# Seven pairs per down projection in layers two to four, with four of the seven weight sums built by adding transfers

## The chip, the cores and the metric

The kernel runs on one core of one Trainium2 chip. The metric is the device time of one execution in microseconds (us), lower is better. Three runs of the kernel before gave a median of 1669.83 us (1669.68 to 1669.99).

## The reference, cut to what matters

The input is 256 tokens of width 1024 in float32. Two blocks follow each other. The first holds four feed-forward layers (counted from 0 in the code: layers 0 to 3), with a state-space mixer between layers 0 and 1 and a neighbourhood attention between layers 2 and 3. Each feed-forward layer is

```
def swiglu(x, w_gu, w_down):
    g, u = jnp.split(x @ w_gu, 2, axis=-1)
    return (jax.nn.silu(g) * u) @ w_down
...
h = h + 0.5 * swiglu(rmsnorm(h, ffn1_norm[i]), ffn1_w_gu[i], ffn1_w_down[i])
```

with `w_gu` of 1024 x 5632 and `w_down` of 2816 x 1024. The change concerns the product with `w_down` (the down projection) of layers 1, 2 and 3.

## The kernel before, in words

**Numbers.** Every float32 product is made of three matmuls of halves: an operand x is split into a rounded part (`hi`) and the rest (`lo`), and hi\*hi + hi\*lo + lo\*hi is summed in PSUM. Weights are loaded from HBM in tiles of up to 2048 columns on 128 partitions (1 MB) into one of four slots of `raw` (`NRAW = 4`). For each tile ScalarE (ACT) writes `whi`, then VectorE (DVE) writes `wlo = raw - whi`; each has three slots (`NSPL = 3`). TensorE (PE) then multiplies. All tiles stand in one list (`plan_of`), and every engine goes through that list in order. ACT may convert tile n once PE has given back tile n-3 (event `w_rel`), and PE needs `wlo` of tile n. SyncE (SP) loads the raw slots in the same order; a slot is free when `w_hi` and `w_lo` of its last tile are done.

**The down projection.** The 2816 rows are 22 blocks of 128 (k), the 1024 columns two halves (c), the 256 tokens two halves (t). An ordinary tile ("rest", label `("down", i, c, y)`) holds up to four blocks k of one column half; each block needs two products of 128x512 (one per t), so six matmuls. A *pair* j takes the blocks 2j and 2j+1 in both column halves, a 2 by 2 block product, by a seven-product scheme (`seven`): 7 products, 21 matmuls, where the plain way takes 8 products, 24 matmuls. For that, sums of weight blocks are needed: the tile `paired` (P_j below; three blocks of the weights themselves, 1536 columns, three products, 9 matmuls) and the tile `mixed` (M_j; three sums of blocks and one block, 2048 columns, four products, 12 matmuls). DVE makes the sums of M_j in `sums`, three dependent additions into a buffer `ts`, just ahead of its `wlo` of P_j. The activations need differences too: POOL makes them (`differences` into `dsum`) in the up projection, and ACT and DVE split them into `dThi` and `dTlo`.

Each layer uses four pairs (blocks 0 to 7). `down_tiles` sets the order: rest (0,0), P0, M0, rest (1,0), P1, M1, rest (0,1), P2, M2, rest (1,1), P3, M3, rest (0,2), and three closing tiles. Between two pairs there is thus an ordinary tile of 24 matmuls (12 after the last pair). The up projection ahead of it runs over 11 chunks of 256 columns, each two tiles of 24 matmuls.

**State space.** Between layers 0 and 1, `w_in` of the mixer passes through 32 tiles (`SSD_TILES`). POOL adds six blocks of squares (`ssd`, into `gate`) late in this stage, and PE reads their total in `square_rows`.

Of the kernel before, what the change touches and what calls it, by code (L numbers as in the profile page):

```python
# [20 lines left out]
PAIRS = 4  # L21
# [141 lines left out]
def plan_of(dr):  # L163
    p = Plan()

    def ffn(i, up, down, extra=None):
        for c in range(11):
            if extra is not None and c in (0, 2):
                p.add(("pproj", extra, c // 2), [wsrc(dr["ple_w_proj"][extra], 0, 2, c * 256, 512)], 2, 512)
            for k in range(2):  # L170
                p.add(("up", i, c, k), [wsrc(up, 4 * k, 4, x * 2816 + c * 256, 256) for x in range(2)], 4, 512)

        def rest(c, y):
            k0, nk = DOWN_TILES[c, y]
            p.add(("down", i, c, y), [wsrc(down, k0, nk, c * 512, 512)], nk, 512)

        for what, x in DOWN_ORDER:
# [5 lines left out]
        for x in DOWN_LAST:  # L183
            rest(*x)
# [78 lines left out]
DOWN_ORDER, DOWN_TILES, DOWN_LAST = down_tiles(PAIRS)  # L263
# [130 lines left out]
def programs(dr, mem, banks, plan, ev):  # L394
# [26 lines left out]

    def wsource(n):

        if labels[n][0] == "mixed":
            return mem[f"ts{labels[n][2] % 3}"][:, :]
        return mem["raw"][:, plan.raw_of[n] % NRAW, columns_of_tile(n)]

    def landed(n):

        if labels[n][0] == "mixed":  # L430
            return at("tsum", *labels[n][1:])
        return at(f"d_w{plan.raw_of[n] % NRAW}", n)
# [120 lines left out]
    def sync(S):  # L553
# [67 lines left out]
    def tensor(T):  # L621
# [203 lines left out]
        def mixed_down(i, r, turn_last):  # L825
# [17 lines left out]
            def rest(c, y):  # L843
                k0, nk = DOWN_TILES[c, y]
# [10 lines left out]
            def seven(j):  # L855
                first, final = j == 0, j == PAIRS - 1
# [19 lines left out]
            for what, x in DOWN_ORDER[1:]:  # L876
# [6 lines left out]
            closing_block([("down", i) + DOWN_LAST[0]], (6, 7), aThi, aTlo, DOWN_TILES[DOWN_LAST[0]][0])  # L883
            residual_in(r, 0, (6, 7))
            held, k0 = [], DOWN_TILES[DOWN_LAST[1]][0]
            for x in DOWN_LAST[1:]:
                hi, lo = take("down", i, *x)
                held += [(hi[:, k, :], lo[:, k, :]) for k in range(DOWN_TILES[x][1])]
            T.wait_ge(*at("aTlo", i, 10))
            for t in range(2):  # L890
                for k, (hi, lo) in enumerate(held):
# [7 lines left out]
                    if t and k == DOWN_TILES[DOWN_LAST[1]][1] - 1:  # L899
                        last.then_inc(*sig(*named(("down", i) + DOWN_LAST[1])))  # L900
                last.then_inc(*sig(*half(("down", i) + DOWN_LAST[2], t)))
# [637 lines left out]
    def scalar(A):  # L1539
# [71 lines left out]
        def ffn(i, r, extra=None):  # L1611
            fa, aThi = mem["fa"], mem["aThi"]

            def high_a(c):
                A.wait_ge(*at("turn_a", i, c))
                b = banks[4 + c % 2]
                if c >= PAIRS:
# [15 lines left out]
            def mixed_down(r):  # L1633
                take("down", i, 0, 0)
                high_a(10)
                for what, x in DOWN_ORDER[1:]:
# [5 lines left out]
                A.wait_ge(*at("w_rel", "paired", i, PAIRS - 1))  # L1642
                copy(flat(mem["ftmp"][:, :, :]), banks[0], scale=0.5).then_inc(*sig("root", i))
                take("down", i, *DOWN_LAST[0])
                take("down", i, *DOWN_LAST[1])
# [5 lines left out]
                take("down", i, *DOWN_LAST[2])  # L1651
# [6 lines left out]
            for c in range(11):  # L1658
# [15 lines left out]
                if 1 <= c <= PAIRS:  # L1674
# [451 lines left out]
    def vector(V):  # L2126
# [8 lines left out]
        def sums(n):  # L2135
# [9 lines left out]
            else:  # L2145
                V.wait_ge(*at("dTlo", i, PAIRS - 1))
# [71 lines left out]
        def ffn(i, r, extra=None):  # L2218
            fa, aThi, aTlo = mem["fa"], mem["aThi"], mem["aTlo"]

            def low_a(c):
                V.wait_ge(*at("aThi", i, c))
                b = banks[4 + c % 2]
                if c >= PAIRS:
# [12 lines left out]
            def merged():  # L2237
# [4 lines left out]
                V.wait_ge(*at("w_rel", "mixed", i, PAIRS - 1))  # L2242
# [8 lines left out]
            def mixed_down(r):  # L2251
                take("down", i, 0, 0)
                low_a(10)
                for what, x in DOWN_ORDER[1:]:
# [5 lines left out]
                take("down", i, *DOWN_LAST[0])  # L2260
                merged()
                V.wait_ge(*at("h21", i))
                for t in range(2):
                    residual(r, t, 0, half(("down", i) + DOWN_LAST[0], t), 6 + t, 0.5)
                take("down", i, *DOWN_LAST[1])
                early_quarters(r)
                V.wait_ge(*at("h22", i))
                for t in range(2):
                    residual(r, t, 1, half(("down", i) + DOWN_LAST[2], t), 2 + t, 0.5)
# [5 lines left out]
                take("down", i, *DOWN_LAST[2])  # L2275
# [7 lines left out]
            for c in range(11):  # L2283
# [14 lines left out]
                if 1 <= c <= PAIRS:  # L2298
# [487 lines left out]
    def gpsimd(G):  # L2786
# [85 lines left out]

        def ffn(i, extra=None):
# [12 lines left out]
        rstds(1)  # L2886
        ssd()
# [8 lines left out]
        ffn(3, 1)  # L2896
        rstds(7)
# [8 lines left out]
def layout(nc):  # L2906
# [44 lines left out]
    put("dThi", [P, PAIRS, 3, P], F32R, a0)  # L2951
    put("dTlo", [P, PAIRS, 3, P], F32R, z + 56 * 1024)
# [108 lines left out]
```

## Time and profile before

| | |
|---|---|
| median of three runs | 1669.83 us |
| the profiled execution | 1669.54 us, of which the span is 1667.7 us |
| mean granted clock of TensorE | 0.998 |
| PE busy | 99% of the span |
| DVE, ACT, POOL busy | 70%, 56%, 8% |
| bytes read from HBM | 297.96 MB |
| down projections of layers 0 to 3 | from about 137, 603, 811 and 1121 us, some 60 us each |
| up projection of layer 0; state-space stage | before 137 us; about 196 to 470 us |

The span is the profiled part of the execution; 1.84 us lie around it. PE's busy time is the union of its matmuls, whose ends are modelled and overlap, so a short wait of PE shows as less idle time than it costs; the starts of successive matmuls tell its pace.

### The profile page before, as it was taken

The page shows a single profiled execution, that of the slowest core. Times are in us where ns is not written, and L with a number is a line of the kernel's source. Part 1 is how long each engine was busy: PE and PEld are TensorE (multiplying, and loading weights), DVE is VectorE, ACT ScalarE, POOL GpSimd, SP SyncE. Part 2 cuts the span into 40 slices and gives each one's busy share as a digit, 9 for nine tenths or more (in the row PEclk, how much of TensorE's full clock was granted, in tenths as well). Part 3 has the DMA queues.
Part 4 walks back from the last instruction along what each step waited for, and adds up shares of the span by engine and source line. Part 5 has one row for each costly group of instructions (what it writes and reads, how often), then busy time and mean ns, then how long its engine had stood idle before and what let it go on. Part 6 is the DMA issues. An engine that isn't in the chain of part 4 may idle for free.

```text
span 1667.7 us, 23289 instructions
## 1 busy us (share of the span) xinstructions
PE 1655.8 (99%) x9318; PEld 1416.7 (85%) x9318; DVE 1161.4 (70%) x1500; ACT 940.5 (56%) x1363; POOL 125.1 (8%) x135
## 2 busy tenths in 40 slices
PE   8999999999999999999999999999999999999998
PEld 7888899999788888888888778888889999988886
DVE  5657878999966568765688767567855578776643
ACT  6545566777865445754456666545653556564532
POOL 0100000000111000010007401000000000000000
PEclk9999999999999999999999999999999999999999
DMA  9654677676556646656487336655655533465551
GB/s 302 194 183 164 186 187 208 180 196 207 161 190 197 195 158 204 200 178 194 159 228 244 114 111 205 190 184 163 220 182 165 161 102 127 156 210 178 177 195 57
DMA packets 244235, 300.58 MB, mean 180 GB/s; under 512 B 9505, under 2 KB 175777, under 8 KB 244129
## 3 DMA queue, kind: packets, MB, share of 16 engines
q1 hardware_dynamic: 238480, 289.26, 54.6%
q10 hardware_dynamic: 5648, 9.85, 2.4%
q8 instruction: 74, 1.21, 0.3%
q14 instruction: 33, 0.26, 0.0%
HBM read 297.96 MB, written 1.11 MB: 179 GB/s over the span
## 4 chain that ended last, share of the span: by engine, by line
PE 98%; DVE 1%; DMA 0%; ACT 0%; issue 0%; DVEq 0%; ACTq 0%
PE bank L625 95%; PE bank L628 4%; DMA prm<-in_prm 0%; DVE wlo L2130 0%; ACT hThi L1546 0%; DVE rTlo L2133 0%; DVE hTlo L2133 0%; DVE xn L2133 0%; DVE h L2133 0%; ACT rThi L1546 0%; DVE xn L2200 0%; DVEq L2988 0%; ACT xn L1543 0%; ACT whi L1546 0%; ACTq L2086 0%
## 5 line engine op out<-in xcount | busy, mean ns | idle before, releaser
L2130 DVE TENSOR_TENSOR wlo<-raw,whi 128x2048 fp32r<-128x2048 f32 (+2 forms) x284 | 613.5, 2165 | 231.1 <-ACT whi L1546 231.1
L1546 ACT ACTIVATE whi<-raw 128x2048 fp32r<-128x2048 f32 (+2 forms) x284 | 511.7, 1810 | 167.1 <-PE bank L625 162.7
L625 PE MATMUL bank<-whi,hThi 128*128 128x512 f32 x1056 | 420.8, 398 | 0.5 <-ACT whi L1546 0.5
L625 PE MATMUL bank<-wlo,hThi 128*128 128x512 f32 x1056 | 412.4, 390 | 0.4 <-DVE wlo L2130 0.4
L625 PE MATMUL bank<-whi,hTlo 128*128 128x512 f32 x1056 | 396.9, 391 | 0.0
L625 PE MATMUL bank<-hThi,whi 128*128 128x256 f32 x888 | 253.4, 285 | 0.0
L625 PE MATMUL bank<-hThi,wlo 128*128 128x256 f32 x888 | 251.2, 283 | 0.0
L625 PE MATMUL bank<-hTlo,whi 128*128 128x256 f32 x888 | 251.2, 283 | 0.0
L625 PEld LDWEIGHTS bank<-whi,hThi 128*128 128x128 f32 x1056 | 198.8, 188 | 44.8 <-issue 5.8
L625 PEld LDWEIGHTS bank<-whi,hTlo 128*128 128x128 f32 x1056 | 198.6, 188 | 42.4
L625 PEld LDWEIGHTS bank<-wlo,hThi 128*128 128x128 f32 x1056 | 198.8, 188 | 40.3 <-DVE wlo L2130 1.5
L625 PEld LDWEIGHTS bank<-hThi,whi 128*128 128x128 f32 x888 | 169.5, 191 | 3.8 <-issue 3.3
L625 PEld LDWEIGHTS bank<-hTlo,whi 128*128 128x128 f32 x888 | 169.5, 191 | 0.2
L625 PEld LDWEIGHTS bank<-hThi,wlo 128*128 128x128 f32 x888 | 169.5, 191 | 0.2
L625 PE MATMUL bank<-whi,aThi 128*128 128x512 f32 x288 | 113.6, 395 | 0.4
L625 PE MATMUL bank<-whi,aTlo 128*128 128x512 f32 x288 | 112.2, 390 | 0.0
L625 PE MATMUL bank<-wlo,aThi 128*128 128x512 f32 x288 | 112.1, 389 | 0.0
L1543 ACT ACTIVATE ftmp<-bank,st 128x256 f32<-128x256 f32 x88 | 41.5, 476 | 101.5 <-PE bank L625 101.5
L2130 DVE TENSOR_TENSOR aTlo<-bank,aThi 128x512 fp32r<-128x512 f32 (+2 forms) x60 | 29.3, 511 | 78.5 <-ACT aThi L1546 78.5
L1546 ACT ACTIVATE aThi<-bank 128x512 fp32r<-128x512 f32 (+2 forms) x60 | 25.5, 457 | 98.3 <-PE bank L628 98.3
L2790 POOL TENSOR_TENSOR st<-st,cst 128x1 f32<-128x1 f32 (+2 forms) x35 | 36.9, 1068 | 458.6 <-DVE st L2173 433.5
L1546 ACT ACTIVATE hThi<-bank,prm 128x128 fp32r<-128x128 f32 (+1 forms) x152 | 43.4, 379 | 47.5 <-PE bank L628 42.4
(245 smaller groups left out, 2157.0 us busy)
## 6 DMA issues: line engine op xcount, KB each, us to landing
raw<-in_ffn_w_gu SPq DMA_DIRECT2D x172, 512.0 KB, 4.8
raw<-in_w_in SPq DMA_DIRECT2D x30, 1024.0 KB, 5.1
raw<-in_ffn_w_down SPq DMA_DIRECT2D x24, 1024.0 KB, 5.1
raw<-in_ffn_w_down SPq DMA_DIRECT2D x40, 512.0 KB, 4.0
raw<-in_ssd_w_in SPq DMA_DIRECT2D x16, 1024.0 KB, 5.7
raw<-in_ssd_w_in SPq DMA_DIRECT2D x32, 512.0 KB, 5.6
raw<-in_w_up SPq DMA_DIRECT2D x16, 1024.0 KB, 5.4
raw<-in_w_down SPq DMA_DIRECT2D x16, 1024.0 KB, 5.1
```

The source lines that it names most:

```text
L625: return T.e.matmul(out, lhsT, rhs, start=start, stop=stop, skip_group_check=skip)
L628: return T.e.transpose(out, in_, ident)
L1543: return e.activation(out, in_, func, **kw)
L1546: return e.activation(out, in_, ACT.Identity, **kw)
L2130: return e.tensor_tensor(out, a, b, op)
L2790: return e.tensor_tensor(out, a, b, op)
```

## The change

`PAIRS` becomes a tuple: layer 0 keeps four pairs, layers 1 to 3 have seven (blocks 0 to 13). `down_tiles` then leaves one ordinary tile in front (rest (0,0), blocks 14 to 17), one of half size (rest (1,0), blocks 14 and 15) after pair 0, and pairs 1 to 6 stand one after the other.

For the pairs in `AHEAD` (1, 2, 4 and 5 of each of the three layers) DVE makes no sums. A new tensor `mix` in HBM holds them; POOL fills it by six transfers for each pair (`mix`: three copies and three transfers with `accum_op` add, each waiting for the one before), 72 in all, one at each "beat": 10 in the up projection of layer 0, 30 in the state-space stage (ahead of POOL's own sums there), and 11, 11 and 10 in the up projections of layers 1 to 3. SP loads such an M_j from `mix` into a raw slot as one transfer of 1 MB, and of P_j only the three blocks that are used (0.75 MB instead of 1 MB). For pairs 0, 3 and 6 DVE still makes the sums, all three in `ts0`.

```
-PAIRS = 4
+PAIRS = (4, 7, 7, 7)
+AHEAD = ((), (1, 2, 4, 5), (1, 2, 4, 5), (1, 2, 4, 5))
+BEATS = (range(1, 11), range(11), range(11), range(11))
+SSD_BEATS = (1, 31, 1)
+MIX = [(i, j) for i in range(4) for j in AHEAD[i]]
...
-                p.add(("mixed", i, x), None, 4, 512)
+                p.add(("mixed", i, x), [dr["mix"][i, x]] if x in AHEAD[i] else None, 4, 512)
...
+    def summed_here(n):
+        return labels[n][0] == "mixed" and labels[n][2] not in AHEAD[labels[n][1]]
...
-                if labels[m][0] == "paired":
+                if labels[m][0] == "paired" and summed_here(m + 1):
                     S.wait_ge(*at("tsum", *labels[m][1:]))
+            if labels[n][0] == "paired" and not summed_here(n + 1):
+                e.dma_start(slot[:, 1:2, 0:512], pieces[0][:, 1:2, :]).then_inc(*sig(f"d_w{q % NRAW}", n, by=16))
+                e.dma_start(slot[:, :, 512:1024], pieces[1]).then_inc(*sig(f"d_w{q % NRAW}", n, by=16))
+                return
+            if labels[n][0] == "mixed":
+                S.wait_ge(*at("m_step", *labels[n][1:], 5))
...
-                if labels[n][0] == "paired":
+                if labels[n][0] == "paired" and summed_here(n + 1):
                     sums(n)
...
+        def mix(i, j, step):
...
+            if step == 0:
+                done = e.dma_start(target[:, 0:2, :], block(0, 1).to_broadcast([P, 2, 512]))
+            elif step == 1:
+                done = e.dma_start(target[:, 0:2, :], diagonal, accum_op=ALU.add)
+            elif step == 2:
+                done = e.dma_start(target[:, 2:3, :], target[:, 0:1, :])
+            elif step == 3:
+                done = e.dma_start(target[:, 2:3, :], block(1, 1), accum_op=ALU.add)
+            elif step == 4:
+                done = e.dma_start(target[:, 3:4, :], target[:, 2:3, :])
+            else:
+                done = e.dma_start(target[:, 3:4, :], block(1, 0), accum_op=ALU.add)
+            done.then_inc(*sig("m_step", i, j, step, by=16))
...
+        def mix_at(n):
+            b = next(beats, None)
+            if b is not None:
+                G.wait_ge(*at("w_hi", n))
+                if b:
+                    G.wait_ge(*at("m_step", *steps[b - 1]))
+                mix(*steps[b])
...
         def ffn(i, extra=None):
-            for c in range(PAIRS):
-                differences(i, c)
+            for c in range(11):
+                if c < PAIRS[i]:
+                    differences(i, c)
...
+                if c in BEATS[i]:
+                    mix_at(tile["up", i, c, 0])
...
         rstds(1)
+        for k in range(*SSD_BEATS):
+            mix_at(tile[SSD_TILES[k]])
         ssd()
```

On DVE, in the middle of a down projection of layers 1 to 3, the rows before read as follows (from M0 on: M0, the fresh column `aTlo`, rest (1,0), the sums and `wlo` of pair 1, `wlo` of M1, rest (0,1)).

```order
L2130 TENSOR_TENSOR wlo<-ts_74,whi 128x2048
L2130 TENSOR_TENSOR aTlo<-bank,aThi 128x512
L2130 TENSOR_TENSOR wlo<-raw,whi 128x2048
L2130 TENSOR_TENSOR ts_75<-raw 128x1024
L2130 TENSOR_TENSOR ts_75<-ts_75,raw 128x512 x2
L2130 TENSOR_TENSOR wlo<-raw,whi 128x1536
L2130 TENSOR_TENSOR wlo<-ts_75,whi 128x2048
L2130 TENSOR_TENSOR wlo<-raw,whi 128x2048
```

The same place now, from `aTlo` on: rest (1,0), pairs 1 and 2 without sums, the sums of pair 3, P3, M3, then P4.

```order
L2143 TENSOR_TENSOR aTlo<-bank,aThi 128x512
L2143 TENSOR_TENSOR wlo<-raw,whi 128x1024
L2143 TENSOR_TENSOR wlo<-raw,whi 128x1536
L2143 TENSOR_TENSOR wlo<-raw,whi 128x2048
L2143 TENSOR_TENSOR wlo<-raw,whi 128x1536
L2143 TENSOR_TENSOR wlo<-raw,whi 128x2048
L2143 TENSOR_TENSOR ts_74<-raw 128x1024
L2143 TENSOR_TENSOR ts_74<-ts_74,raw 128x512 x2
L2143 TENSOR_TENSOR wlo<-raw,whi 128x1536
L2143 TENSOR_TENSOR wlo<-ts_74,whi 128x2048
L2143 TENSOR_TENSOR wlo<-raw,whi 128x1536
```

The sums of an inner pair now stand between two pairs instead of behind an ordinary tile of 2048 columns.

On POOL, from the end of layer 0 through the state-space stage, only the six sums stood before, after the last additions of the layer and the norm.

```order
L2790 TENSOR_TENSOR h<-h,ftmp 128x512
L2790 TENSOR_TENSOR h<-h,fa 128x512
L2790 TENSOR_TENSOR st<-st,cst 128x1 x2
L2790 TENSOR_TENSOR gate<-gate 128x512 x6
L2790 TENSOR_TENSOR st<-st,cst 128x2
```

Now 30 transfers stand between the norm and the sums; these are the last six of them and what follows.

```order
L2902 DMA mix<-mix 128x512
L2904 DMA mix<-in_ffn_w_down 128x512
L2894 DMA mix<-in_ffn_w_down 128x2x512
L2896 DMA mix<-in_ffn_w_down 128x2x512
L2898 DMA mix<-mix 128x512
L2900 DMA mix<-in_ffn_w_down 128x512
L2803 TENSOR_TENSOR gate<-gate 128x512 x6
L2803 TENSOR_TENSOR st<-st,cst 128x2
```

POOL's sums are now behind all 30 transfers in its queue.

## Rows read from the trace of the kernel before

**Rows 1.** The page, part 1: busy us, share, instructions of each engine.

```profile
PE 1655.8 (99%) x9318; PEld 1416.7 (85%) x9318; DVE 1161.4 (70%) x1500; ACT 940.5 (56%) x1363; POOL 125.1 (8%) x135
```

**Rows 2.** Busy us by stretch: layer 1's down stage, its up stage, state space.

```profile
core 0: us, PE busy (x) PEld busy (x) DVE busy (x) ACT busy (x) POOL busy (x), PEclk, DMA share, GB/s
...
603.00:663.00 60.00, 59.88 (x270) 49.02 (x269) 48.06 (x47) 32.42 (x31) 3.00 (x2) 1.00 0.58 193
...
560.00:600.00 40.00, 40.00 (x186) 33.09 (x185) 22.39 (x18) 17.50 (x18) 0.00 (x0) 1.00 0.58 191
...
200.00:411.00 211.00, 210.91 (x1714) 205.55 (x1714) 189.91 (x299) 150.25 (x233) 0.55 (x1) 1.00 0.69 193
```

**Rows 3.** Timeline of PE in layer 1's down stage: start, us, engine, line, operation.

```profile
613.47 0.39 PE L625 MATMUL bank<-whi,aTlo 128*128 128x512 f32 x1
613.98 0.47 PE L625 MATMUL bank<-whi,aThi 128*128 128x512 f32 x1
614.29 0.39 PE L625 MATMUL bank<-wlo,aThi 128*128 128x512 f32 x1
...
616.14 0.39 PE L625 MATMUL bank<-whi,aThi 128*128 128x512 f32 x1
...
619.54 0.39 PE L625 MATMUL bank<-whi,aThi 128*128 128x512 f32 x1
...
624.07 0.39 PE L625 MATMUL bank<-whi,aTlo 128*128 128x512 f32 x1
```

**Rows 4.** Timeline of DVE in the same stage.

```profile
611.54 2.29 DVE L2130 TENSOR_TENSOR wlo<-raw,whi 128x2048 fp32r<-128x2048 f32 x1 [1.11 <-ACT whi L1546]
613.75 1.22 DVE L2130 TENSOR_TENSOR ts<-raw 128x1024 f32<-128x1024 f32 x1
615.00 1.42 DVE L2130 TENSOR_TENSOR ts<-ts,raw 128x512 f32<-128x512 f32 x2
616.34 1.75 DVE L2130 TENSOR_TENSOR wlo<-raw,whi 128x1536 fp32r<-128x1536 f32 x1
...
621.75 2.29 DVE L2130 TENSOR_TENSOR wlo<-raw,whi 128x2048 fp32r<-128x2048 f32 x1 [1.05 <-ACT whi L1546]
```

**Rows 5.** Timeline of ACT in the same stage.

```profile
609.60 3.28 ACT L1546 ACTIVATE whi<-raw 128x2048 fp32r<-128x2048 f32 x2
616.45 1.92 ACT L1546 ACTIVATE whi<-ts 128x2048 fp32r<-128x2048 f32 x1 [3.57 <-DVE ts L2130]
619.80 3.54 ACT L1546 ACTIVATE whi<-raw 128x2048 fp32r<-128x2048 f32 x2 [1.43 <-PE bank L625]
621.84 1.50 ACT L1546 ACTIVATE whi<-raw 128x1536 fp32r<-128x1536 f32 x1
```

**Rows 6.** The busiest 10 us of the transfers, and issues with median us to landing.

```profile
870.00:880.00 10.00, 10.00 (x50) 8.26 (x49) 5.56 (x13) 6.61 (x15) 1.07 (x2) 1.00 1.04 374
...
raw<-in_ffn_w_down SPq DMA_DIRECT2D x24, 1024.0 KB, 5.1
raw<-in_ffn_w_down SPq DMA_DIRECT2D x40, 512.0 KB, 4.0
...
tb<-in_rpb SPq DMA_DIRECT2D x2, 1000.0 KB, 14.1
...
out<-xn SPq DMA_DIRECT2D x4, 256.0 KB, 2.1
```

**Rows 7.** State space: ACT's second and thirty-first tile, POOL's sums, PE's read of them.

```profile
199.84 1.93 ACT L1546 ACTIVATE whi<-raw 128x2048 fp32r<-128x2048 f32 x1
...
380.07 1.90 ACT L1546 ACTIVATE whi<-raw 128x2048 fp32r<-128x2048 f32 x1
...
411.10 1.29 POOL L2790 TENSOR_TENSOR gate<-gate 128x512 f32<-128x512 f32 x1 [209.64 <-DVE EW L2130]
...
457.02 3.21 POOL L2790 TENSOR_TENSOR gate<-gate 128x512 f32<-128x512 f32 x1 [3.97 <-ACT gate L1543]
...
465.24 1.50 PE L625 MATMUL bank<-cst,gate 128*128 128x2 f32 x13
```

More of the change, by code:

```diff
@@ L173, in rest @@
         def rest(c, y):
-            k0, nk = DOWN_TILES[c, y]
+            k0, nk = DOWN_TILES[i][c, y]
             p.add(("down", i, c, y), [wsrc(down, k0, nk, c * 512, 512)], nk, 512)
-        for what, x in DOWN_ORDER:
+        for what, x in DOWN_ORDER[i]:
             if what == "rest":
@@ L855, in seven @@
             def seven(j):
-                first, final = j == 0, j == PAIRS - 1
+                first, final = j == 0, j == PAIRS[i] - 1
                 hi, lo = take("paired", i, j)
@@ L875, in mixed_down @@
             clear(0, 1, 2, 3, 5)
-            for what, x in DOWN_ORDER[1:]:
+            for what, x in DOWN_ORDER[i][1:]:
                 if what == "rest":
@@ L882, in mixed_down @@
                 empties[b] = (event, i)
-            closing_block([("down", i) + DOWN_LAST[0]], (6, 7), aThi, aTlo, DOWN_TILES[DOWN_LAST[0]][0])
+            closing_block([("down", i) + DOWN_LAST[i][0]], (6, 7), aThi, aTlo, DOWN_TILES[i][DOWN_LAST[i][0]][0])
             residual_in(r, 0, (6, 7))
-            held, k0 = [], DOWN_TILES[DOWN_LAST[1]][0]
-            for x in DOWN_LAST[1:]:
+            held, k0 = [], DOWN_TILES[i][DOWN_LAST[i][1]][0]
+            for x in DOWN_LAST[i][1:]:
                 hi, lo = take("down", i, *x)
-                held += [(hi[:, k, :], lo[:, k, :]) for k in range(DOWN_TILES[x][1])]
+                held += [(hi[:, k, :], lo[:, k, :]) for k in range(DOWN_TILES[i][x][1])]
             T.wait_ge(*at("aTlo", i, 10))
@@ L898, in mixed_down @@
                         turn(1, 0, 1)
-                    if t and k == DOWN_TILES[DOWN_LAST[1]][1] - 1:
-                        last.then_inc(*sig(*named(("down", i) + DOWN_LAST[1])))
-                last.then_inc(*sig(*half(("down", i) + DOWN_LAST[2], t)))
+                    if t and k == DOWN_TILES[i][DOWN_LAST[i][1]][1] - 1:
+                        last.then_inc(*sig(*named(("down", i) + DOWN_LAST[i][1])))
+                last.then_inc(*sig(*half(("down", i) + DOWN_LAST[i][2], t)))
             residual_in(r, 1, (2, 3))
@@ L1635, in mixed_down @@
                 high_a(10)
-                for what, x in DOWN_ORDER[1:]:
+                for what, x in DOWN_ORDER[i][1:]:
                     if what == "rest":
@@ L1650, in mixed_down @@
                     high(1, 0, 1)
-                take("down", i, *DOWN_LAST[2])
+                take("down", i, *DOWN_LAST[i][2])
                 if r == 1:
@@ L2253, in mixed_down @@
                 low_a(10)
-                for what, x in DOWN_ORDER[1:]:
+                for what, x in DOWN_ORDER[i][1:]:
                     if what == "rest":
@@ L2259, in mixed_down @@
                     take("mixed", i, x)
-                take("down", i, *DOWN_LAST[0])
+                take("down", i, *DOWN_LAST[i][0])
                 merged()
@@ L2263, in mixed_down @@
                 for t in range(2):
-                    residual(r, t, 0, half(("down", i) + DOWN_LAST[0], t), 6 + t, 0.5)
-                take("down", i, *DOWN_LAST[1])
+                    residual(r, t, 0, half(("down", i) + DOWN_LAST[i][0], t), 6 + t, 0.5)
+                take("down", i, *DOWN_LAST[i][1])
                 early_quarters(r)
@@ L2268, in mixed_down @@
                 for t in range(2):
-                    residual(r, t, 1, half(("down", i) + DOWN_LAST[2], t), 2 + t, 0.5)
+                    residual(r, t, 1, half(("down", i) + DOWN_LAST[i][2], t), 2 + t, 0.5)
                     if r == 1 and t == 0:
@@ L2274, in mixed_down @@
                     scaled(0)
-                take("down", i, *DOWN_LAST[2])
+                take("down", i, *DOWN_LAST[i][2])
                 if r == 1:
@@ L2871, in differences @@
             tt(d[:, 384:512], a[:, 256:384], d[:, 256:384], ALU.subtract).then_inc(*sig("dsum", i, c))
+        def mix(i, j, step):
+            w = dr["ffn1_w_down" if i % 2 == 0 else "ffn2_w_down"][i // 2]
+            block = lambda k, c: w[256 * j + 128 * k:256 * j + 128 * k + 128, 512 * c:512 * c + 512].unsqueeze(1)
+            first = block(0, 0)
+            diagonal = bass.AP(first.tensor, first.offset, [[D, P], [P * D + 512, 2], [1, 512]])
+            target = dr["mix"][i, j]
+            if step == 0:
[11 more added lines that the diff above has]
+            done.then_inc(*sig("m_step", i, j, step, by=16))
+        steps = [(i, j, step) for i, j in MIX for step in range(6)]
+        beats = iter(range(len(steps)))
+        def mix_at(n):
[5 more added lines that the diff above has]
+                mix(*steps[b])
         def ffn(i, extra=None):
-            for c in range(PAIRS):
-                differences(i, c)
+            for c in range(11):
+                if c < PAIRS[i]:
+                    differences(i, c)
                 if c == 2 and extra is not None:
                     ple_rstd(extra)
+                if c in BEATS[i]:
+                    mix_at(tile["up", i, c, 0])
             G.wait_ge(*at("h12p", i))
@@ L2896, in gpsimd @@
         ffn(3, 1)
+        assert next(beats, None) is None
         rstds(7)
```

38 lines of the change are left out of this document (20 added, 18 removed).

## The prediction

> **What bounds the kernel now.** I read the page first: PE is busy 99% of the span, the other engines 70% and less [rows 1]. So the time falls only by what PE no longer does, and rises by every wait that PE gets. Next the busy time by stretch: in layer 1's down stage PE is busy 59.88 of 60 us, DVE 48.06 and ACT 32.42 [rows 2]; the stages of layers 2 and 3 read alike. The reader should see that DVE has only a fifth of this stage free, while in the up stage it has nearly half (22.39 of 40 us). Last the timelines of the three engines in this stage, because an average hides which wait ends last.
>
> PE's pace comes from starts: from 616.14 to 624.07 us there are 35 steps without a wait, 0.2266 us each [rows 3]. (The 0.39 us of a row is the length of one pipelined matmul, not the pace.) A pair of 21 matmuls thus takes 4.76 us, its P_j 2.04, its M_j 2.72, an ordinary tile of 24 takes 5.44.
>
> **What is removed.** Nine more pairs (three in each of three layers) save three matmuls each: 27 x 0.2266 = 6.1 us, all of it on PE, so on the path. A second, small gain: in the stage before, the matmul due at 613.70 (613.47 + 0.23) starts at 613.98, and the next follows after 0.31 instead of 0.23 [rows 3]. This is rest (1,0), whose conversion could start on ACT only at 609.60 [rows 5] and ended on DVE at 611.54 + 2.29 = 613.83 [rows 4]. The tile now has half the columns; at half the durations (an estimate: 0.96 on ACT, 1.15 on DVE) it would be ready near 611.8. That removes 0.28 + 0.08 = 0.36 us per layer, 1.1 us in three.
>
> **What is moved: the sums between two pairs.** This is the step on which I decide. Between two pairs there was an ordinary tile of 5.44 us of PE work; from pair 1 to pair 6 there is none. Take the latencies from the rows: ACT starts 0.26 us after PE's next tile has started (619.54 to 619.80), converts 2048 columns in 1.92, DVE starts 0.03 later and its next instruction follows 2.21 after (611.54 to 613.75); the sums take 2.59 (613.75 to 616.34); `wlo` of P takes 1.75; PE starts 0.15 after `wlo` (613.83 to 613.98) [rows 3 to 5].
>
> Count from the moment when PE ends P1. M2 is three tiles behind P1, so ACT may convert it then: 0.26 + 1.92 + 0.03 + 2.21 = 4.42 when DVE is free. DVE takes its instructions in order, and behind `wlo` of M2 stand the sums of pair 3: to 7.01. Then `wlo` of P3: to 8.76; PE could start P3 at 8.91. PE has only M1, P2 and M2 to do meanwhile, 33 x 0.2266 = 7.48. P3 comes 1.43 us late, with 0.08 for the restart 1.51. Next M3: ACT can start it when the sums are done, 2.70 after they began (616.45 - 613.75), at 7.12; + 1.92 + 0.03 + 2.29 + 0.15 = 11.51. PE would have reached it at 8.99 + 2.04 = 11.03: late by 0.48, with the restart 0.56. One inner summed pair thus costs 2.07 us. Pair 6 stands in the same place behind pairs 4 and 5; pair 0 keeps its place. Two per layer, six in all: 12.4 us.
>
> What is late next: P4 and M4 are converted behind M3, but PE is then late itself, and the same count leaves them 1.2 and 0.7 us to spare. Behind pair 6 comes a tile whose conversion may start well before, and PE's wait gives ACT and DVE time.
>
> A pair summed ahead must hold pace too. M_j may be converted when P_(j-1) ends: 0.26 + 1.92 + 0.03 + 2.29 + 0.15 = 4.65 us, against 4.76 of PE work: 0.11 to spare. P_j: 0.26 + 1.50 + 0.03 + 1.75 + 0.15 = 3.69 against 4.76. Both hold, M_j barely: if the latencies were 0.1 longer than read, each could cost up to 0.1, all twelve 1.2 us.
>
> **What is added elsewhere, at no cost.** In the up stage three more chunks per layer get POOL's differences and their split; ACT has 22 and DVE 18 of 40 us free there [rows 2]. The beats in the up stages come once per chunk, 48 x 0.2266 = 10.9 us apart, so POOL waits for a step only if it takes longer; then the differences, ACT's split and what is queued behind it on ACT would be late. SP's wait for the last step of a pair would hold up all weight loads behind it, but the steps end stages earlier; only in layer 3 are the last ones issued in its own up stage, two chunks and half a down stage ahead. SP's table for the attention now waits for M6 of layer 2 instead of M3, which comes about when the slot for the next load is freed anyway.
>
> **The loads.** A pair summed ahead needs 0.75 + 1 MB (1.835 million bytes) in 4.76 us, 385 GB/s; the highest rate over 10 us was 374 [rows 6], and this stage itself moved 193 GB/s at a share of 0.58 [rows 2], 333 when busy. So four slots must bridge. The tightest is M2: its slot is rest (1,0)'s, free near 611.9 on the old stage's clock; ACT wants M2 when P1 ends, at 613.70 + 21 x 0.2266 (rest (1,0) and P1) + 0.26 = 618.7. That is 6.8 us for a load that takes 5.1 [rows 6]. The summed pairs need only 1 MB in more than 6 us. I take no wait; the price if that is wrong is 1.835/333 or /374 against 4.76: 0.75 or 0.15 us for each of twelve pairs, 9.0 or 1.8 us.
>
> The Trainium skill's page "DMA: Bandwidth & Descriptors" (Specifications) gives 358 GB/s as the limit of HBM for a core. By that an ahead pair takes 5.13 us, 4.4 us more in twelve if nothing were buffered, and the sum would be 1679.4. The 374 GB/s of the trace is over this limit, so the trace decides.
>
> **The steps in the state-space stage.** The trace has no adding transfer. Its nearest rows: 2.1 us for a 256 KB store below, 14.1 us for the slowest load of 1000 KB above [rows 6]. The steps move 256 or 512 KB, and an adding one reads as much again; the rows nearest to this are the loads of 512 KB (4.0) and 1 MB (5.1). I take 5. What they must meet: the first can be issued at 201.8 (second tile's `whi`), and the thirtieth's gate falls at 382 [rows 7]. POOL's six sums come behind, five of 1.29 and one of 3.21, 9.7 us, and PE reads them at 465.2 [rows 7]. So 29 steps have till 455.5: 8.75 us each. At 5 they just follow the tiles and cost nothing; above 8.75, each us costs 29. Weight loads have a share of 0.69 there and DVE is busy 190 of 211 us [rows 2], but the steps take nothing from DVE.
>
> By the Trainium skill's page "DMA: Bandwidth & Descriptors" (Anatomy of one DMA — SWDGE (gpsimd) path), a transfer issued by POOL takes 2.0 us + bytes/436e3, by estimate 2.6 and 3.2 us for the two sizes; by it the sum stays as it is. No row of this trace shows it.
>
> **The sum.** - 6.1 - 1.1 + 12.4 = + 5.2 us. On the profiled 1669.54 that gives 1674.7; the median is 0.29 higher, so 1675.0 for a median. A change is told from none here at 0.2%, 3.3 us.
>
> **The rivals.**
> - *Loads fall behind as well* (14%): the 385 GB/s are not bridged. For it: the demand is above every rate of the trace. Against: 1.7 us to spare in the tightest place. 1677 to 1684.
> - *The waits are half as long* (14%): then + 6.2 - 7.2 = - 1.0, about 1669, no change. For it: they are differences of long chains, 8.91 against 7.48. Against: the latencies agree from place to place.
> - *The sums find room and the gain is kept* (10%): the mechanism is that DVE has pair 3's sums done before PE needs P3; it decides at a chain of 7.48 us instead of 8.91, if DVE could have M2's `wlo` behind it 1.4 us sooner. Then - 7.2, 1662.6. For it: DVE's work for pairs 1 to 6, 4 x 3.96 + 2 x 6.55 = 28.9 us (2.21 + 1.75 each, 2.59 more with sums), nearly fits into PE's 28.6. Against: three slots don't let it work ahead.
> - *The steps are late in the state-space stage* (6%): at 10 us each + 36 us, near 1711.
> - The forecast has 56%; its own range is 1673 to 1677 (from waits of 1.8 to 2.4 us per inner summed pair), of which 6 points lie within 0.2%.
>
> Faster 10%, same 14 + 6 = 20%, slower 70%. The range from 1669.5 to 1682 leaves out the kept gain, the late steps and the far end of late loads, some 20%.
>
> **What would show it.** In the new timeline PE should wait near 1.4 us before P3 and P6 and 0.5 before M3 and M6 in layers 1 to 3, released by `wlo`, and not before pairs 1, 2, 4, 5; DVE's sums should begin the moment `wlo` of the tile ahead ends. Pace and matmul count: 27 matmuls fewer at 0.2266. Steps should land within 4 to 7 us, and POOL's sums end before 455. The prediction is wrong if PE waits for transfers, or if `wlo` comes before PE asks for it.

## The result, and the profile after

The changed kernel takes 1683.79 us (median of 4 runs, 1680.80 to 1685.09) against 1669.76 (1668.97 to 1669.99) of the kernel before: a ratio of 1.0082 [1.0068, 1.0096], slower by 14.0 us. The forecast was 1675.0 with a range to 1682: the direction is right, the size is 8.8 us too small and outside the range. The profiled execution is the fastest of the four, 1680.80 us with a span of 1679.0, 11.3 us above the one of before. In the table further down, single executions far above the rest (2350 us of steps alone, 5344 of fetch later, three of the kernel before beside some of the runs) are left out of the ratios, and move no median by more than 0.15 us.

The page of the kernel after, part 1, and in part 3 the queue of POOL's transfers (packets, MB, share), which before did not exist:

```profile
PE 1654.0 (99%) x9291; PEld 1412.8 (84%) x9291; DVE 1179.1 (70%) x1527; ACT 963.2 (57%) x1408; POOL 191.8 (11%) x234
q0 software_dynamic: 10368, 25.17, 8.2%
```

Against [rows 1], PE has 27 matmuls fewer, as counted. Its busy time fell by 1.8 us only, because the busy time is a union of overlapping lengths; starts tell more. The first and the last matmul of layer 1's down stage (whose operands are `aThi` and `aTlo`), of before:

```profile
603.03 0.39 PE L625 MATMUL bank<-whi,aThi 128*128 128x512 f32 x1
661.82 0.39 PE L625 MATMUL bank<-whi,aTlo 128*128 128x512 f32 x1
```

and of after, with PE's two longest waits and the matmul ahead of each (columns as in [rows 3]):

```profile
608.56 0.39 PE L638 MATMUL bank<-whi,aThi 128*128 128x512 f32 x1
...
631.31 0.39 PE L638 MATMUL bank<-whi,aTlo 128*128 128x512 f32 x1
632.88 0.47 PE L638 MATMUL bank<-whi,aThi 128*128 128x512 f32 x1 [1.18 <-issue]
...
634.80 0.40 PE L638 MATMUL bank<-whi,aTlo 128*128 128x512 f32 x1
635.52 0.47 PE L638 MATMUL bank<-whi,dThi 128*128 128x512 f32 x1 [0.33 <-DVE wlo L2143]
...
669.06 0.39 PE L638 MATMUL bank<-whi,aTlo 128*128 128x512 f32 x1
```

The stage begins 5.53 us later than before and takes 60.50 us instead of 58.79. Layers 2 and 3 read alike (60.49 for 58.77, 60.44 for 58.76). So the 11.3 us of the profiled execution are 5.5 before the first of the three stages, 5.1 in them (1.7 each), and 0.7 elsewhere. Half of the loss is where the prediction looked for it, the other half where it put a cost of nothing.

**The down stage** went as counted. DVE's timeline of after, from `wlo` of M2 on:

```profile
626.23 2.29 DVE L2143 TENSOR_TENSOR wlo<-raw,whi 128x2048 fp32r<-128x2048 f32 x1 [0.71 <-ACT whi L1559]
628.43 1.22 DVE L2143 TENSOR_TENSOR ts<-raw 128x1024 f32<-128x1024 f32 x1
629.69 1.42 DVE L2143 TENSOR_TENSOR ts<-ts,raw 128x512 f32<-128x512 f32 x2
631.02 1.75 DVE L2143 TENSOR_TENSOR wlo<-raw,whi 128x1536 fp32r<-128x1536 f32 x1
633.09 2.29 DVE L2143 TENSOR_TENSOR wlo<-ts,whi 128x2048 fp32r<-128x2048 f32 x1 [0.31 <-ACT whi L1559]
```

The sums of pair 3 begin when `wlo` of M2 ends, `wlo` of P3 ends at 632.77, and PE starts P3 0.11 us later. PE's step there is 632.88 - 631.31 = 1.57 us instead of 0.23, and at M3 0.72 (with 0.30 for the step behind each). That is 1.99 us for an inner summed pair, where the prediction had 2.07; pair 6 shows the same.

**The state-space stage** did not go as counted. ACT's timeline of before behind its third tile (ACTq rows are transfers that ACT issues):

```profile
227.41 0.34 ACTq L1766 DMA_DIRECT2D cum<-ct  x1
229.81 0.92 ACTq L1759 DMA_DIRECT2D Er<-cum  x2
230.77 1.92 ACT L1546 ACTIVATE whi<-raw 128x2048 fp32r<-128x2048 f32 x1 [3.40 <-DMA cum<-ct]
```

and of after, where POOL had issued the fourth step of this stage, 512 KB, at 226.45:

```profile
227.43 0.34 ACTq L1779 DMA_DIRECT2D cum<-ct  x1
232.82 0.92 ACTq L1772 DMA_DIRECT2D Er<-cum  x2
233.78 1.91 ACT L1559 ACTIVATE whi<-raw 128x2048 fp32r<-128x2048 f32 x1 [6.38 <-DMA cum<-ct]
```

ACT stores 64 KB of cumulative sums to HBM (`column_sums`) and then fetches parts of them in another layout, 512 KB in each transfer (`fetch`); it waits for the store before it issues the fetch. The store landed in 2.4 us before and in 5.4 us now. The windows of the store, of before and of after:

```profile
227.50:230.00 2.50, 2.50 (x23) 2.50 (x22) 2.50 (x7) 0.00 (x0) 0.00 (x0) 1.00 0.56 107
227.50:232.80 5.30, 5.30 (x46) 5.30 (x45) 3.40 (x9) 0.00 (x0) 0.09 (x1) 1.00 1.07 213
```

Beside the step the DMA engines are full (share 1.07 instead of 0.56; the last number is GB/s). The conversion `whi` stands behind this wait in ACT's order, and PE behind the conversion: `whi` starts 3.01 us later than before (233.78, 230.77), and PE idles as long. PE's row, and the windows around it:

```profile
238.12 0.55 PE L638 MATMUL bank<-hThi,whi 128*128 128x256 f32 x1 [3.00 <-issue]
```

```profile
core 0: us, PE busy (x) PEld busy (x) DVE busy (x) ACT busy (x) POOL busy (x), PEclk, DMA share, GB/s
230.00:238.00 8.00, 5.12 (x43) 4.92 (x41) 3.17 (x5) 4.22 (x6) 0.58 (x1) 0.97 1.05 264
238.00:241.00 3.00, 2.88 (x13) 2.91 (x14) 3.00 (x10) 1.01 (x1) 0.00 (x0) 0.50 1.00 189
241.00:245.00 4.00, 4.00 (x36) 4.00 (x35) 3.42 (x4) 3.10 (x4) 0.84 (x1) 1.00 0.82 287
```

PE idles for 3.0 us, and then works at a granted clock of 0.50 (1.2 instead of 2.4 GHz) until nearly 241, 13 matmuls in 3 us where the window behind has 9 per us. Those 13 would have taken some 1.4 us at that pace, so the slow clock costs some 1.4 us more (an estimate). From 242 on the stage runs 4.25 us behind before (ACT's ninth `whi` there starts at 246.31 instead of 242.06). The rest comes near its end, where another fetch lands late (8.55 us; the one at the same place of before took 6.32), beside a step issued 0.13 us after it:

```profile
421.92 0.69 DVE L2143 TENSOR_TENSOR Er<-Er,later 128x512 f32<-128x512 f32 x1 [1.93 <-DMA Er<-cum]
```

The steps themselves, in this stage (KB each, median us to landing):

```profile
mix<-in_ffn_w_down POOLq DMA_DIRECT2D x10, 512.0 KB, 8.2
mix<-mix POOLq DMA_DIRECT2D x10, 256.0 KB, 5.9
mix<-in_ffn_w_down POOLq DMA_DIRECT2D x10, 256.0 KB, 7.1
```

From the first (202.10) to the thirtieth (436.17) they are 8.07 us apart, and the DMA share from 200 to 411 us is 0.89, not 0.69 [rows 2].

### The profile page after: what moved, and what is told of

It reads as the page before. It is cut to its first block, busy times and chain, and to the rows that moved or that the text cites. A ratio compares the mean times of both kernels' runs of the same rounds, so it can differ in the third digit from the quotient of the medians.

```text
span 1679.0 us, 23537 instructions
## 1 busy us (share of the span) xinstructions
PE 1654.0 (99%) x9291; PEld 1412.8 (84%) x9291; DVE 1179.1 (70%) x1527; ACT 963.2 (57%) x1408; POOL 191.8 (11%) x234
## 4 chain that ended last, share of the span: by engine, by line
PE 87%; DVE 6%; ACT 3%; issue 1%; DMA 1%; POOL 1%; ACTq 0%; DVEq 0%
PE bank L638 84%; PE bank L641 4%; DVE wlo L2143 2%; ACT whi L1559 2%; DVE ts L2143 1%; DVE EW L2143 1%; DMA Er<-cum 1%; POOL bm L2803 0%; POOL st L2803 0%; DVE bc L2146 0%; DMA h<-in_x 0%; DMA cum<-ct 0%; DVE xTs L2146 0%; ACT hThi L1559 0%; DVE xTs L2143 0%
## 5 line engine op out<-in xcount | busy, mean ns | idle before, releaser
L2143 DVE TENSOR_TENSOR wlo<-raw,whi 128x2048 fp32r<-128x2048 f32 (+3 forms) x296 | 639.0, 2164 | 230.1 <-ACT whi L1559 230.0
L1559 ACT ACTIVATE whi<-raw 128x2048 fp32r<-128x2048 f32 (+3 forms) x296 | 531.4, 1801 | 176.1 <-PE bank L638 168.5
L638 PE MATMUL bank<-whi,aThi 128*128 128x512 f32 x252 | 99.9, 396 | 7.2 <-issue 7.1
L638 PE MATMUL bank<-whi,aTlo 128*128 128x512 f32 x252 | 98.3, 390 | 0.0
L638 PE MATMUL bank<-wlo,aThi 128*128 128x512 f32 x252 | 98.1, 389 | 0.0
L2143 DVE TENSOR_TENSOR aTlo<-bank,aThi 128x256 fp32r<-128x256 f32 (+2 forms) x69 | 28.7, 447 | 76.9 <-ACT aThi L1559 76.9
L2146 DVE SCALAR_TENSOR_TENSOR hTlo<-bank,prm,hThi 128x128 fp32r<-128x128 f32 (+1 forms) x152 | 42.8, 351 | 34.6 <-ACT hThi L1559 34.6
```

The lines of the kernel that those rows point to most:

```text
L638: return T.e.matmul(out, lhsT, rhs, start=start, stop=stop, skip_group_check=skip)
L1559: return e.activation(out, in_, ACT.Identity, **kw)
L2143: return e.tensor_tensor(out, a, b, op)
L2146: return e.scalar_tensor_tensor(out, a, s, b, op0, op1)
```

## The experiments

All medians stand beside runs of the kernel before of the same batch, 1669.4 to 1669.9 us.

| kernel | median us | ratio to before |
|---|---|---|
| no steps | 1674.47 | 1.0029 [1.0018, 1.0040] |
| no inner sums | 1676.28 | 1.0042 [1.0027, 1.0057] |
| small steps | 1676.77 | 1.0042 [1.0027, 1.0057] |
| steps moved | 1676.90 | 1.0043 [1.0029, 1.0058] |
| six pairs | 1675.25 | 1.0037 [1.0023, 1.0051] |
| sums cut | 1664.74 | 0.9967 [0.9956, 0.9979] |
| store guarded | 1679.79 | 1.0060 [1.0043, 1.0078] |
| steps alone | 1678.13 | 1.0048 [1.0032, 1.0064] |
| POOL sums, six pairs | 1694.99 | 1.0156 [1.0140, 1.0171] |
| POOL sums, seven pairs | 1715.41 | 1.0274 [1.0260, 1.0288] |
| fetch later | 1675.72 | 1.0034 [1.0020, 1.0048] |

**No steps.** M_j of the pairs summed ahead is loaded from other weights of the same size.

```
-p.add(("mixed", i, x), [dr["mix"][i, x]] if x in AHEAD[i] else None, 4, 512)
+p.add(("mixed", i, x), [up[0:P, 0:2048].rearrange("p (a b) -> p a b", a=4)] if x in AHEAD[i] else None, 4, 512)
...
-if labels[n][0] == "mixed":
-    S.wait_ge(*at("m_step", *labels[n][1:], 5))
...
-steps = [(i, j, step) for i, j in MIX for step in range(6)]
+steps = []
```

> All 72 adding and copying steps are left out, and each mixed tile summed ahead is loaded from a plain piece of the up weights (same size, one transfer of 1 MB); the result is not the reference's. Theory (the loss is the waits of PE in the down stages, 1.7 us per layer, plus a state-space stage in which the steps' traffic delays the small transfers cum<-ct and Er<-cum): the down stages still take 1.7 us more each, the state-space stage takes what it took before, 1675 us in all, some 9 us under the changed kernel's median. Rival (the state-space stage is slower for another reason than the steps): its 5.6 us stay, 1680 us.

Measured 1674.47, on the prediction's sum. The state-space stage is back (layer 1's down stage begins at 603.42), and the down stages take 60.4 to 60.7 us as in the changed kernel. So the steps cost 9.3 us in the median, and seven pairs alone 4.6.

**Steps alone.** The other half: four pairs everywhere, all 72 steps at their beats, into a tensor that nothing reads.

```
-PAIRS = (4, 7, 7, 7)
+PAIRS = (4, 4, 4, 4)
-AHEAD = ((), (1, 2, 4, 5), (1, 2, 4, 5), (1, 2, 4, 5))
+AHEAD = ((), (), (), ())
-MIX = [(i, j) for i in range(4) for j in AHEAD[i]]
+MIX = [(i, j) for i in (1, 2, 3) for j in (1, 2, 4, 5)]
```

> Four pairs in every layer with DVE's sums, as in the kernel before, but all 72 adding steps are issued at the changed kernel's beats into a tensor that nothing reads. The computation is whole. Theory (steps and down stages cost independently): 1669.8 plus the 9.3 us that lie between the changed kernel and the one without steps: about 1679; gate of the state-space stage shifted by 5 to 6 us in the profile, down stages 59.0 us each as before, except where steps run in them. Rival (the two costs share something, such as late steps delaying the loads of the sums): 1672 to 1676.

Measured 1678.13, 8.3 us above before; the down stages take 58.80 us each. The two costs add: 4.6 + 8.3 = 12.9 of 14.0. In this trace the store took 6.9 us and PE idled longer:

```profile
240.01 0.55 PE L638 MATMUL bank<-hThi,whi 128*128 128x256 f32 x1 [4.55 <-issue]
```

The stage was 7.3 us late behind it, and its end 8.3 us.

**Small steps.** All 72 transfers, each on 16 of 128 rows; M_j loaded as in the kernel with no steps.

```
...
-target = dr["mix"][i, j]
+target = dr["mix"][i, j][0:16]
...
```

> All 72 steps at their places with their waits, but each on 16 of the 128 rows (an eighth of the bytes); mixed tiles are loaded from plain weights, so the sums are left out and the result is not the reference's. Theory (the steps' traffic is what delays the small transfers): cum<-ct lands in about 2.4 us as before and the time is that of the run without steps, 1675 us. Rival (POOL's issuing or its place in the queue costs, whatever the size): the state-space stage keeps its 5.6 us, 1680 us or more.

The state-space stage is not late (layer 1's down stage begins at 603.0), and the store lands in 2.1 us beside a step of 64 KB. POOL issues as many steps in the same order, and an issue takes it nearly as long (in the median 0.77 us for one from `in_ffn_w_down`, 0.82 in the changed kernel). So it is what the steps move that delays, and not POOL's issuing, nor its order by itself; whether their bytes (an eighth in this stage) or their packets (a quarter), this run doesn't tell apart.

The median is 2.3 us above the kernel with no steps, and that lies behind the computation. In the traces PE's last matmul starts no later (1665.53, with no steps 1666.07) and the last store lands no later (1672.42 and 1672.97). But POOL's closing instruction, a DRAIN (durations in ns), here ends at 1674.68, behind that store. It, and the one of the kernel with no steps:

```profile
L3042 POOLq DRAIN  x1: 6992/6992/6992, 1667.7 to 1667.7; - x1
L3040 POOLq DRAIN  x1: 1089/1089/1089, 1668.2 to 1668.2; - x1
```

In the changed kernel it takes 4.54 us and ends 0.19 us ahead of the last store's landing, so there it costs nothing. Why it takes longest behind the small steps stays open.

**Steps moved.** The whole computation, with 13 steps in the state-space stage instead of 30, the others as second beats in the up stages.

```
-SSD_BEATS = (1, 31, 1)
+SSD_BEATS = (8, 21, 1)
+TWICE = (range(4, 11), range(7, 11), range(7, 11), range(7, 9))
...
+if c in TWICE[i]:
+    mix_at(tile["up", i, c, 1])
```

> The whole computation. Only the beats move: 13 steps in the middle of the state-space stage (tiles 8 to 20), so that none is in flight when cum<-ct is stored and none in the stage's last part where Er<-cum is fetched again and again; the others become second beats in the later chunks of the up stages. Theory (the loss there is a collision with those small transfers): the state-space stage is back within 1 us of before, 1675 to 1676 us. Rival (it is the volume of traffic in the stage, spread over it): 13 of 30 steps leave 13/30 of 5.6 us, 2.4 us, 1677 to 1678; if second beats delay POOL's differences, more.

1676.90: the store takes 2.0 us, the stage is on time (603.2), and 6.9 us come back. The time is still 0.9 us above the theory's 1675 to 1676: layer 1's down stage takes 62.0 us instead of 60.5. Three steps still run there, and M2 lands late (ACT waits 2.11 us for `raw<-mix`, and PE 1.26 for this tile).

**Store guarded.** One wait of POOL ahead of the fourth step of the stage.

```
+if n == tile[SSD_TILES[4]]:
+    G.wait_ge(*at("d_cs"))
```

> The changed kernel with one wait more: POOL issues the fourth adding step of the state-space stage only when the small store cum<-ct has landed. The computation is whole. Theory (the stage is late because that store and the fetch Er<-cum are slow beside a step in flight): the store lands in 2.4 us again, PE's 3.0 us idle near 238 us and the slow matmuls behind it are gone, 4.2 us fewer; the second collision near 413 us stays, 1.2 to 1.4 us: about 1679.5. Rival (the traffic slows the whole stage, the store is only where it shows): the wait comes up at another place, at most 1 us fewer, 1683.

The median fell by 4.0 us, as the theory has it, and the store landed in 2.9 us. PE's idle time there:

```profile
236.13 0.36 PE L638 MATMUL bank<-hThi,whi 128*128 128x256 f32 x1 [0.56 <-issue]
```

But the profiled run doesn't settle it: behind this place the stage is only 0.5 us later than ahead of it, and near its end it then loses 4.9 us, where the changed kernel lost 1.3. PE waits 0.49 us at 426.61 and 2.26 at 439.31, both for DVE's `EW`, and from 440.5 to 443.5 the granted clock is 0.50. In the chain ahead of the second wait there are two things. A fetch beside a step takes 9.48 us (6.32 in before), and DVE waits 2.87 us for it. Then POOL's sums, which had stood behind the steps, run beside DVE's work, on POOL and then on DVE:

```profile
427.20 3.25 POOL L2803 TENSOR_TENSOR gate<-gate 128x512 f32<-128x512 f32 x2
...
427.38 1.94 DVE L2143 TENSOR_TENSOR xTs<-xTs,gate 128x512 f32<-128x512 f32 x1
429.24 1.76 DVE L2143 TENSOR_TENSOR Er<-Er,cst 128x512 f32<-128x512 f32 x1
```

Each of these two DVE instructions takes 0.69 us elsewhere. In the changed kernel one of them meets POOL's sums (1.48 us at 440.13). The prediction had "the steps take nothing from DVE"; in this trace their place ahead of POOL's sums does.

**Fetch later.** The wait is left and its place in ACT's order is moved: the first two fetches are issued one tile later, behind a conversion. All 72 steps stay.

```
                if i == 2:
                    column_sums()
+               if i == 3:
                    fetch(0)
                    fetch(1)
```

> The changed kernel with two lines moved on ACT: the first two fetches of Er<-cum are issued one tile later, so that ACT has converted the next tile before it waits for the small store cum<-ct. All 72 steps stay where they are. The computation is whole. Theory (the store is slow beside a step, and what costs is that ACT stands in its queue for it with a conversion behind): the store still takes about 5 us or more, but PE's idle near 238 us and the slow clock behind it are gone; about 4 us fewer, near 1679.7; the later collision of Er<-cum stays. Rival (the traffic itself is the price, through the weight loads): at most 1 us fewer, 1683.

1675.72, 8.1 us fewer, twice what was expected. ACT's timeline:

```profile
228.11 0.34 ACTq L1779 DMA_DIRECT2D cum<-ct  x1
228.50 1.92 ACT L1559 ACTIVATE whi<-raw 128x2048 fp32r<-128x2048 f32 x1 [0.42 <-ACT ct L1559]
...
233.81 1.08 ACTq L1772 DMA_DIRECT2D Er<-cum  x2
```

The store still takes 5.7 us, and the DMA load is as heavy (the 1 MB weight loads of the stage take 7.5 us in the median, 5.6 before). But the conversion now runs while the store is under way, PE has no wait, and layer 1's down stage begins at 603.49, 0.46 us later than before. At the later fetches DVE waits 0.67 us, and it costs nothing by the stage's end. So at the store the traffic by itself is hidden; what costs is that ACT stands in its order waiting for a small transfer. (In the kernel with no steps PE has no wait there, so the move by itself had nothing to gain.) That the loss near the stage's end went too is luck as far as this run shows: it was not forecast, nothing in the edit aims at it, and it wasn't tried by itself. (POOL's late sums meet DVE there too, 1.30 instead of 0.69 us at 435.06, without a wait of PE.)

**Sums cut.** No steps, and DVE's additions for pairs 3 and 6 cut to four columns.

```
+if few:
+    tt(o[:, 0:4], w[:, 512:516], w[:, 0:4], ALU.add).then_inc(*sig("tfirst", i, j))
     ...
```

> The kernel without steps (1674.5), but DVE's three additions for pairs 3 and 6 of layers 1 to 3 are cut to four columns each; everything else, the loads of these pairs as full tiles too, stays. Left out: most of the sums of those pairs. Theory (the waits are DVE's additions in the chain behind M2 and M5): the chain to P3 falls from 8.91 to 6.3 us against 7.48 of PE work, no wait is left, some 12 us fewer: about 1662.5. Rival (the loads take the place of DVE as the limit, as they did when all six inner pairs were summed ahead): 1667 to 1673, with ACT waiting for raw tiles.

1664.74, 9.7 us fewer than with no steps and 5.1 under before; stages of 56.6, 56.7 and 57.4 us. Between DVE's rows for M2 and P3 there are now 0.46 us, not 2.59:

```profile
620.99 2.29 DVE L2141 TENSOR_TENSOR wlo<-raw,whi 128x2048 fp32r<-128x2048 f32 x1 [0.71 <-ACT whi L1557]
623.20 0.15 DVE L2141 TENSOR_TENSOR ts<-raw 128x4 f32<-128x4 f32 x1
...
623.66 1.75 DVE L2141 TENSOR_TENSOR wlo<-raw,whi 128x1536 fp32r<-128x1536 f32 x1
```

PE's step at P3 and M3 of layers 1 and 2 is 0.45 us at most, not 1.57 and 0.72. So DVE's additions are the cause in the down stage, and seven pairs would gain if these cost nothing. The next three kernels try to take them away.

**No inner sums.** No steps, and all six pairs behind the first loaded as if summed ahead.

```
+AHEAD = ((), (1, 2, 3, 4, 5, 6), (1, 2, 3, 4, 5, 6), (1, 2, 3, 4, 5, 6))
```

> As the run without steps, and DVE also makes no sums for pairs 3 and 6: six pairs in a row, each with 0.75 + 1 MB of loads, 385 GB/s asked of the transfers. Sums are left out, so the result is not the reference's. Theory (DVE's sums between two pairs make the waits, 2.07 us each): no wait of PE is left in the down stages, 1662.6 us, 7.2 under before. Rival (the loads are the limit): PE waits for transfers in the down stages, 0.15 to 0.75 us per pair, 1665 to 1676 us.

1676.28: the rival, just above its range. DVE's additions are gone and the time is not better, because ACT waits for tiles. Windows of layer 1's down stage, and an ACT row of M6:

```profile
603.00:623.00 20.00, 20.00 (x92) 16.50 (x91) 13.54 (x10) 11.87 (x9) 0.00 (x0) 1.00 0.54 186
623.00:633.00 10.00, 10.00 (x46) 8.07 (x44) 7.52 (x5) 7.03 (x5) 0.00 (x0) 1.00 1.01 358
633.00:643.00 10.00, 9.25 (x42) 7.47 (x41) 6.57 (x4) 5.36 (x4) 0.00 (x0) 1.00 0.90 317
643.00:653.00 10.00, 8.35 (x37) 6.59 (x36) 9.14 (x7) 5.26 (x4) 0.00 (x0) 1.00 1.00 352
```

```profile
641.07 1.92 ACT L1557 ACTIVATE whi<-raw 128x2048 fp32r<-128x2048 f32 x1 [2.48 <-DMA raw<-in_ffn_w_gu]
```

At a share of 1.0 the stage moves 352 to 358 GB/s, under the 385 that these pairs ask for. The buffers bridge three of these pairs; from the fourth on (M4 in each of the three layers) PE waits. The Trainium skill's page "DMA: Bandwidth & Descriptors" (Specifications) gives about 358 GB/s for a core. These windows are near it, but the trace of before moves 386 GB/s from 872 to 882 us, at a share of 1.05, so no trace here shows 358 as a limit that holds everywhere.

**Six pairs.** The whole computation, the steps as in the kernel with moved steps.

```
+PAIRS = (4, 6, 6, 6)
+AHEAD = ((), (2, 3, 4, 5), (2, 3, 4, 5), (2, 3, 4, 5))
```

> Six pairs instead of seven in layers 1 to 3; pairs 2 to 5 are summed ahead, pairs 0 and 1 by DVE, so that no summed pair stands behind another pair without an ordinary tile of full (0,0) or half size between. The adding steps keep the thinned beats of the kernel with moved steps. The computation is whole. Theory (the down stages lose by the two inner summed pairs alone): no wait of 1.5 and 0.5 us is left; against the kernel before six pairs save 3 x 2 x 3 matmuls x 0.2266 = 4.1 us, and the steps cost some 1.5 us where they still run in layer 1's down stage: about 1667. Rival (with four pairs ahead in a row the loads are the limit, as with all six inner pairs summed ahead): 1670 to 1674, waits of ACT for raw tiles in the second half of each down stage.

1675.25, the rival again, and above its range. With four pairs ahead in a row, M5 waits for its load (ACT 2.83 us for `raw<-mix` at 641.32 in layer 1) and PE 1.99 us; the stages take 60.6, 59.9 and 60.0 us.

**POOL's sums.** No steps; DVE sums the first pairs, POOL the others, in the down stage, from full tiles.

```
+            for j in ON_POOL[i]:
+                sums(i, j)
```

> No adding steps and no tensor of sums: six pairs in layers 1 to 3, every pair loaded as one full tile; DVE makes the sums of pairs 0 and 1, POOL those of pairs 2 to 5, in the down stage, as soon as a tile has landed. The computation is whole. POOL's additions by the rows of before: 3.14 us for 1024 columns, 1.30 to 1.74 for 512, so 5.7 to 6.6 us a pair, 23 to 26 us for four; begun near 609 they end at 632 to 635, and M5 must have its sums by 635.5. Theory (what is lost in the down stage is DVE's additions between pairs, and what is lost before it is the steps' traffic; neither is here): six pairs keep their gain of 4.1 us: 1665.7. Rival (POOL's additions slow DVE, or are late, or the loads are the limit again): 1668 to 1675.

> As the kernel with six pairs and POOL's sums, but seven pairs; DVE makes the sums of pair 0, POOL those of pairs 1 to 6. The computation is whole. Theory by the count of the prediction: 1669.8 - 7.2 = 1662.6 if POOL keeps up; six pairs at 5.7 to 6.6 us are 34 to 40 us from about 604, M6 must have its sums by 637.6, so POOL is late by 0.5 to 6 us in each of three layers: 1664 to 1680, and the later pairs wait for POOL, not for DVE. Rival (POOL's additions are faster with whole tiles in place): 1662.6.

1694.99 and 1715.41, both much worse than expected; the stage of layer 1 takes 67.0 and 73.5 us. Timelines of six pairs, POOL and then DVE, over the same 5 us:

```profile
619.32 2.40 POOL L2808 TENSOR_TENSOR ts<-raw 128x1024 f32<-128x1024 f32 x1 [4.37 <-DMA raw<-in_ffn_w_down]
621.80 5.43 POOL L2808 TENSOR_TENSOR ts<-ts,raw 128x512 f32<-128x512 f32 x2
```

```profile
617.41 1.75 DVE L2148 TENSOR_TENSOR wlo<-raw,whi 128x1536 fp32r<-128x1536 f32 x1
619.48 4.40 DVE L2148 TENSOR_TENSOR wlo<-ts,whi 128x2048 fp32r<-128x2048 f32 x1 [0.32 <-ACT whi L1564]
```

`wlo` of 2048 columns takes 4.40 us where it took 2.29 alone: POOL's addition ran from 619.32 to 621.72, and 621.72 + 2.29 = 624.01 is nearly where `wlo` ends (623.88). In the three stages POOL's additions of 512 columns take 2.71 us in the mean, against 1.30 to 1.74 for nearly all of before. So here an addition on POOL doesn't run beside DVE's work, it stands in its place. The Trainium skill's page "SBUF — State Buffer" (SBUF: two separate sides) says that a DVE instruction with two SBUF inputs and a GpSimd instruction that reads SBUF take a shared port pair as an exclusive lock for a whole instruction; the rows of POOL's addition and of `wlo` agree.

No kernel with the whole computation beats the kernel before. The best are six pairs and fetch later, 5 to 6 us slower.

## Why the prediction was right in direction and wrong in size

1. **What is removed: right.** 27 matmuls fewer at the old pace. Rest (1,0)'s wait is gone: no step of PE there is longer than 0.24 us, and the stage lengths fit: 58.79 - 3 x 3 x 0.2266 - 0.36 + 2 x 1.99 = 60.37 against 60.50 measured.
2. **The sums between two pairs: right**, 1.99 us for 2.07, at the two places and in the order forecast. Sums cut shows that DVE's additions cause them: 9.7 us came back of some 12 expected. In its trace the three stages are 10.8 us shorter than with no steps, with one wait for `wlo` (0.61 us) left in layer 3's. Behind layer 2's stage PE then waits 1.48 us at 880.18, for a tile for whose load ACT had waited (0.78 us for `raw<-in_na_w_qkv` at 878.50). So the loads take part of it back.
3. **The pairs summed ahead: right.** With the beats at the places of the change, PE has no wait before pairs 1, 2, 4 and 5. "I take no wait" for the loads holds for two such pairs in a row; no inner sums and six pairs show it fail at the fourth. One reading under it was wrong: 374 GB/s is not the highest rate over 10 us of the trace of before, which from 872 to 882 us is 386, so the 385 asked were not above every rate; but the down stage itself got 352 to 358 when the loads were its limit.
4. **The steps in the state-space stage: the step that failed.** "At 5 they just follow the tiles and cost nothing" held only POOL's chain against its deadline, and put the steps' effect on other transfers at nothing without a reason. They cost 9.3 us in the median (8.3 by themselves in steps alone), and 5.6 in the profiled execution (a span of 1679.0 against 1673.4 with no steps), 4.25 of them at one place. The price of a step was too low as well: they land in 5.9 to 8.2 us in the median and are 8.07 us apart, not 5. But in POOL's chain even this fits under 8.75: POOL's last sum starts at 464.10, takes 3.21, and PE reads it at 470.82 without a wait. (The mark "before 455" could not have been met: in the kernel before the last sum starts at 457.02 [rows 7].) What the prediction left out is what the steps delay. The store `cum<-ct` (64 KB, 2.4 to 5.4 us) and a fetch `Er<-cum` (512 KB, 6.32 to 8.55 us) have users on the path, the store's in the middle of ACT's order. Small steps shows that what the steps move does it, and not their place in POOL's queue by itself; fetch later shows that with the store's wait one tile later in ACT's order the same steps cost 1.2 us of 9.3, though the part near the stage's end is gone there by luck. The rival "steps are late" had the right stage and the wrong mechanism.
5. **Size.** The sum without this step, 1675.0, is what no steps (1674.5) and fetch later (1675.7) measured. How late the stage gets depends on which transfer a step meets. PE's first idle was 0.56, 3.00 and 4.55 us in three kernels whose store took 2.92, 5.36 and 6.91: each time what the store took over 2.36 us, so here its delay reaches PE in full. The three slower runs of the changed kernel (1683.7 to 1685.1) have no trace; that they met a store as slow as in steps alone is not shown. Nor does a run of its own show the cause of the loss near the stage's end (1.3 us in the changed kernel, 4.9 with the store guarded); the late fetch and POOL's late sums are read from timelines.

## What to carry to other kernels

Ahead of adding background transfers, list the transfers whose landing an engine waits for in its own order, the small ones too, and ask what each costs if it takes 3 us longer; a mean share of the DMA engines (0.69 in this stage) doesn't answer that. If such a wait can stand one tile later in the order, much of the cost may go: here 1.2 us were left of 9.3. Where work is taken out of a full pipe, count its fixed work between two tiles (here the sums) against the time that the removed work used to give it, and check in a trace that the engine named to take it over can work beside the one that is relieved.

## What was not expected of the hardware

- A 64 KB store took 1.7 to 2.9 us without a step in flight (DMA share of 0.53 to 0.56 during the store in three of these traces) and 5.4 to 6.9 us with one 512 KB step in flight (1.02 to 1.07).
- After 3.0 us without a matmul the granted clock was 0.50 from 238 to 241 us and 1.00 behind it; in steps alone, after 4.55 us, it was 0.50 from 240 to 245, and in store guarded, after 2.26 us, from 440.5 to 443.5. After 0.56 us, and after the 1.2 us waits of the down stages, it stayed at 1.00.
- DVE's subtraction and POOL's addition on tiles of SBUF did not run side by side: 2.29 us became 4.40.
- POOL's closing DRAIN took 1.09 us with no steps, 4.54 behind 72 steps of full size and 6.99 behind 72 small ones.
